# State updates of the linear attention as two half-tile products over four chunks

## The reference

```python
def gla_chunked(q, k, v, g, s0):          # per chunk of 16 tokens
    b = jnp.cumsum(g, axis=2)
    q_dec, k_inv = q * jnp.exp(b), k * jnp.exp(-b)
    k_end = k * jnp.exp(b_last - b)
    a = jnp.where(causal, jnp.einsum('bnihk,bnjhk->bnhij', q_dec, k_inv), 0.0)
    o_intra = jnp.einsum('bnhij,bnjhv->bnihv', a, v)
    def step(s, xs):
        o = jnp.einsum('bihk,bhkv->bihv', qd, s)
        s = s * dec[..., None] + jnp.einsum('bjhk,bjhv->bhkv', ke, vv)
        return s, o
    ...
```

## Time and profile before

| | us |
|---|---|
| median of 3 runs | 3917.28 (3915.54 to 3919.32) |
| profiled execution, device time | 3916.27 |
| its span in the profile | 3914.5 |
| TensorE busy in it | 3387.8 (87%) |
| VectorE busy | 2694.3 (69%) |
| ScalarE busy | 2125.3 (54%) |
| GpSimd busy | 572.5 (15%) |

### The profile page before, as it was taken

The page is one execution under the profiler, slowest core; times in us unless marked ns, Lnnn a source line. Parts: engine busy times, 40 slices in busy tenths (PEclk is TensorE's granted clock), DMA queues, the critical chain, the costliest instruction groups (busy, mean ns, idle before and its releaser), DMA issues. The chain is left out here.

```text
span 3914.5 us, 50754 instructions
## 1 busy us (share of the span) xinstructions
PE 3387.8 (87%) x17144; PEld 2769.9 (71%) x17144; DVE 2694.3 (69%) x3836; ACT 2125.3 (54%) x2780; POOL 572.5 (15%) x286
## 2 busy tenths in 40 slices
PE   8869999957978999948888987999997888879997
PEld 6757777746766777737777676888776777568875
DVE  3669999966668999976865656774565555555545
ACT  3539999943538999953444623332234445634433
POOL 0005333410004334420020300000000011300000
PEclk9879999978979999978989888999998989789998
DMA  3149999942048999953320032331331210022222
GB/s 111 49 152 396 419 418 410 407 180 94 12 164 356 419 416 416 412 200 117 104 70 2 1 108 100 117 117 65 113 105 50 58 61 1 3 80 96 93 84 81
DMA packets 148091, 651.33 MB, mean 166 GB/s; under 512 B 23478, under 2 KB 36968, under 8 KB 89448
## 3 DMA queue, kind: packets, MB, share of 16 engines
q1 hardware_dynamic: 137576, 631.59, 42.6%
q0 software_dynamic: 10080, 16.80, 1.1%
q10 hardware_dynamic: 288, 1.05, 0.1%
HBM read 645.01 MB, written 24.26 MB: 171 GB/s over the span
## 5 line engine op out<-in xcount | busy, mean ns | idle before, releaser
L1762 DVE TENSOR_TENSOR w_low<-w_raw,w_high 128x2048 fp32r<-128x2048 f32 x392 | 881.9, 2282 | 55.5 <-ACT w_high L1759 51.2
L1759 ACT CAST w_high<-w_raw 128x2048 fp32r<-128x2048 f32 x392 | 746.1, 1910 | 77.5 <-DMA w_raw<-in_moe_gate_dram 33.8
L2069 PE MATMUL banks<-w_high,x_split 128*128 128x512 f32 x1024 | 421.0, 411 | 46.6 <-DVE w_low L1762 39.1
L2069 PE MATMUL banks<-w_low,x_split 128*128 128x512 f32 x1024 | 407.8, 398 | 0.0
L529 PE MATMUL banks<-w_high,x_high 128*128 128x512 f32 (+2 forms) x808 | 309.6, 383 | 57.4 <-DVE w_low L435 31.5
L399 ACT CAST w_high<-w_raw 128x512 fp32r<-128x512 f32 (+2 forms) x200 | 117.8, 589 | 427.1 <-PE banks L529 421.2
L3376 PE MATMUL banks<-x_high,w_high 128*128 128x512 f32 (+1 forms) x1056 | 320.9, 358 | 21.2 <-DVE w_low L3414 21.2
L3376 PE MATMUL banks<-x_high,w_low 128*128 128x512 f32 (+1 forms) x1056 | 324.0, 361 | 0.0
L3376 PE MATMUL banks<-x_low,w_high 128*128 128x512 f32 (+1 forms) x1056 | 320.1, 357 | 0.0
L529 PE MATMUL banks<-w_high,x_low 128*128 128x512 f32 (+2 forms) x808 | 300.3, 372 | 0.0
L529 PE MATMUL banks<-w_low,x_high 128*128 128x512 f32 (+2 forms) x808 | 300.3, 372 | 0.0
(11 more groups left out here) (410 smaller groups left out, 7241.4 us busy)
## 6 DMA issues: line engine op xcount, KB each, us to landing
w_raw<-in_moe_gate_dram SPq DMA_DIRECT2D x132, 1024.0 KB, 10.5
w_raw<-in_moe_up_dram SPq DMA_DIRECT2D x132, 1024.0 KB, 10.2
w_raw<-in_moe_down_dram SPq DMA_DIRECT2D x132, 1024.0 KB, 10.9
w_raw<-in_ffn_w_up_dram SPq DMA_DIRECT2D x44, 1024.0 KB, 4.9
w_raw<-in_ffn_w_down_dram SPq DMA_DIRECT2D x88, 256.0 KB, 2.7
modulation<-in_w_adaT_dram SPq DMA_DIRECT2D x42, 512.0 KB, 4.2
hiddenT<-in_w_adaT_dram SPq DMA_DIRECT2D x28, 512.0 KB, 3.7
w_raw<-in_w_cols_dram SPq DMA_DIRECT2D x48, 256.0 KB, 2.9
```

What stands on the lines that cost most here:

```text
L1759: act.copy(ex["WS"][0][:, v % HIGH, :], ex["WR"][:, v % RAW, :]).then_inc(ex["high"], 1)
L1762: dve.tensor_tensor(ex["WS"][1][:, v % LOW, :], ex["WR"][:, v % RAW, :], ex["WS"][0][:, v % HIGH, :].bitcast(F32), ALU.subtract).then_inc( ...
L2069: ins_ = pe.matmul(GU[b][m], stationary(b, kk), WS[w][:, s, k * BANK:(k + 1) * BANK], start=(kk == 0 and w == 0), stop=(kk == KD - 1 and w ...
```

## The change

The widened values have four chunks in place of eight: the new table `half_chunk` marks, on each partition, the chunk's number within its half of the tile (chunks 0 to 3 on partitions 0 to 63, and 4 to 7 as 0 to 3 on 64 to 127). An update is now two matmuls: partitions 0 to 63 into one bank, 64 to 127 into the next, each with 256 moving columns. Only the second one signals `updates`. Further:

- `UB(n)` is a pair of half-filled banks of 0 to 3, so `BR` is 2; `VX` has 6 buffers of half the size.
- VectorE evacuates direction 0 of n % 3 != 2, that is two halves of three n; ScalarE four.
- VectorE widens only n = 0, ahead of the loop; GpSimd all others, and its three `block_q` come behind all widenings.
- `place` copies from two banks, with four chunks of each.

```diff
+    parts["half_chunk"] = (np.arange(P)[:, None] // CHUNK % 4 == np.arange(4)[None, :]) * 1.0
-        VR, BR, SR = 3, 4, 4
+        VR, BR, SR, NC4 = 6, 2, 4, P // CHUNK // 2
-            VX = spare[:, 0:VR * NC8 * GLA_DV].rearrange("p (r c v) -> p r c v", r=VR, v=GLA_DV)
+            VX = spare[:, 0:VR * NC4 * GLA_DV].rearrange("p (r c v) -> p r c v", r=VR, v=GLA_DV)
-            UB = lambda n: self.ps[0:2 * GLA_DK, n % BR, :]
+            UB = lambda n: self.ps[0:2 * GLA_DK, n % BR * 2:n % BR * 2 + 2, 0:NC4 * GLA_DV]
-            by_dve = lambda n, d: d == 0 and n % 3 == 0
+            by_dve = lambda n, d: d == 0 and n % 3 != 2
-            from_pool = lambda n: n % 3 != 2
+            from_pool = lambda n: n > 0
-                eng.tensor_tensor(VX[:, n % VR], V(n // HG, n % HG).unsqueeze(1).broadcast_to([P, NC8, GLA_DV]),
-                                  self.const("chunk").unsqueeze(2).broadcast_to([P, NC8, GLA_DV]),
+                eng.tensor_tensor(VX[:, n % VR], V(n // HG, n % HG).unsqueeze(1).broadcast_to([P, NC4, GLA_DV]),
+                                  self.const("half_chunk").unsqueeze(2).broadcast_to([P, NC4, GLA_DV]),
-                return copy(dst, UB(n)[d * GLA_DK:(d + 1) * GLA_DK].rearrange("p (c v) -> p v c", v=GLA_DV))
+                return copy(dst.rearrange("p v (b c) -> p v b c", b=2),
+                            UB(n)[d * GLA_DK:(d + 1) * GLA_DK].rearrange("p b (c v) -> p v b c", v=GLA_DV))
-                        if t % 2 == 1:
-                            pool.wait_ge(expanded[0], expands((t + 1) * HG - 2))
-                            block_q(pool.tensor_copy, 0, t // 2).then_inc(blocked, 1)
-                            pool.wait_ge(blocked, t // 2 + 1)
+                    pool.wait_ge(expanded[0], expands(N - 1))
+                    for hh in range(HG):
+                        block_q(pool.tensor_copy, 0, hh).then_inc(blocked, 1)
+                        pool.wait_ge(blocked, hh + 1)
-                        pe.matmul(UB(n), KE[:, n // HG, grp * HG + n % HG].rearrange("p d k -> p (d k)"),
-                                  VX[:, n % VR].rearrange("p c v -> p (c v)"), start=True, stop=True).then_inc(updates, 1)
+                        for b in range(2):
+                            half = slice(b * P // 2, (b + 1) * P // 2)
+                            ins_ = pe.matmul(UB(n)[:, b], KE[half, n // HG, grp * HG + n % HG].rearrange("p d k -> p (d k)"),
+                                             VX[half, n % VR].rearrange("p c v -> p (c v)"), start=True, stop=True)
+                        ins_.then_inc(updates, 1)
-                    expand(dve, 2)
+                    expand(dve, 0)
-                            if n + 3 < N:
-                                expand(dve, n + 3)
```

## The result

| | before | after |
|---|---|---|
| median, us | 3917.57 (3909.57 to 3919.32, 6 runs) | 3891.32 (3888.75 to 3898.29, 6 runs) |
| profiled execution, us | 3916.27 | 3897.15 |
| its span, us | 3914.5 | 3895.3 |

The ratio is 0.9941, with an interval of 0.9929 to 0.9952.

The account below looks back on a forecast made before the run. TensorE was taken to set the pace of the four stages, ScalarE 0.2 us behind. Stage gains of 17.0 us, less 0.9 and 1.2, left 14.9: 3916.3 - 14.9 = 3901.4 us, range 3897 to 3915.

Parts of the forecast that it names:

- The four more constants' columns cost nothing that a row could show.: Constants table: its four added columns were taken to have no visible cost.
- Halves side by side, 0.43 us.: State update on TensorE: two 64-row products overlap, taking 0.43 us at 2.4 GHz instead of 0.86 in a row.
- Rival 3: Half overlap: the second half waits for the first's second pass, 0.64 us a pair; 3909.5 us, chance 0.08.
- The circle: Warm tile: slowest dependency loop, update, scores, three masks, next evacuation on VectorE, next update; 3.04 us instead of 3.38.
- ScalarE's circle: Warm tile: the loop through ScalarE's four evacuations, 2.54 us, below the loop through VectorE.
- Widenings and q copies hidden.: GpSimd: three half widenings of 0.52 us a tile, and q copies of 1.0 to 1.5 us each, delay nothing.
- The evacuations from two banks: Copies out of the paired banks: no change taken, 0.62 and 0.67 us, though 0.1 more each was not excluded.
- The first tile: Cold start of each stage at half clock: loop of 3.66 us, update 5 starting 6.47 us after the stage's start.
- the second stage has some 0.45 less to give: Second stage of each layer: 1.4 us less at half clock, so 0.45 us less gain each, 0.9 in all.
- All of it should reach the end.: Behind the stages: the whole 14.9 us gain arrives at the kernel's end, since nothing late waits there.
- Rival 2: TensorE's clock stays at 1.2 GHz: no stage gain, and products behind start at half rate; 3927 us, chance 0.08.
- Rival 1: The update's halves run one after the other: warm loop 3.47 us, total 3915 to 3918, no difference; chance 0.14.

Follow-up runs that it names:

- pad4: The kernel before with the four half_chunk columns added to its constants table and nothing that uses them; 3901.49 us, ratio 0.9970.
- samewidth: The whole change, but half_chunk takes the place and width of the unused table chunk, so no tile moves; 3910.66 us, ratio 0.9980 to before.
- masks21: The changed kernel with VectorE's order as two masks, the next tile's first evacuation, then the third mask; 3887.53 us, ratio 0.9923 to before.
- acts5: The changed kernel with the moved evacuation given back, so ScalarE does five and VectorE one; 3899.35 us, ratio 0.9974 to before.
- after_again: The changed kernel run once more, unaltered, on the same chip as the other runs; 3894.74 us, ratio 0.9947 to before.

## Why the prediction was wrong, step by step

*"The four more constants' columns cost nothing that a row could show."* This step failed, and it is the miss. They cost nothing where they are read, but move each tile behind them, and 17.7 of the 26 us come from there (pad4). The forecast thought of reading four more columns, and not of a longer table that moves the tiles behind it. With this term taken out, the rest was too high: 8.6 us (samewidth) where 14.9 were forecast. The two misses pull against each other: 17.7 us of gain are missing and 6.3 are too many, so the total is nearer than its parts, by luck.

*Halves side by side, 0.43 us.* Right. From the start of the third update to the scores it takes 2147.33 - 2146.75 = 0.58 us, and 0.43 + 0.09 + 0.05 were summed. Rival 3's 0.64 for a pair would give 0.78: the second half doesn't wait for the first half's second pass.

*The circle.* Right, 3.10 for 3.04: VectorE's order last, with no idle time behind the masks. masks21 and acts5 move it by what the terms say. ScalarE's circle, next in line, was summed too low: 2.54 for the 2.77 of masks21, with no wait in it. The wake of TensorE was 0.08 for 0.05.

*Widenings and q copies hidden.* Right, though a half widening takes 0.61 us on GpSimd where half of 1.04 was taken; the copies take 0.86 each and end 4.5 us ahead of the scans. The evacuations from two banks are unchanged, 0.62 and 0.69.

*The first tile, and "the second stage has some 0.45 less to give".* Wrong in size. In the first stage, where the clock rises as assumed, the first mask follows its scores 1.26 us later (2140.53 to 2141.79) where 0.95 was taken, and the stage comes out at 21.79 for 21.59. In the second stages it was assumed that the clock rises as far into them as before. In after it rises 8.8 us into the second stage of layer 0 and 9.0 into that of layer 1, where the earlier trace rows had 5.4 in the former:

```profile
2199.60:2208.00 8.40, 7.68 (x42) 3.63 (x45) 4.46 (x9) 5.04 (x8) 6.15 (x11) 0.50 0.01 2
2208.50:2221.70 13.20, 10.06 (x99) 4.69 (x96) 10.17 (x23) 10.29 (x18) 6.08 (x9) 1.00 0.00 1
2222.10:2225.10 3.00, 2.92 (x14) 2.96 (x15) 3.00 (x2) 2.95 (x4) 0.00 (x0) 0.50 0.00 0
```

The stage starts at 2199.36. Over the runs of the changed stage its length goes with the rise: 20.7 us with a rise at 4.1 us, 21.2 at 6.5, 22.1 at 9.0, 22.3 at 10.5 (all layer 1). In the second stages 1.2 and 1.8 us are missing from the forecast, 3.0 of the 3.9 missing in all. Where the rise falls is not the change's doing alone: in pad4, whose stages are those of before, the first comes at 4.0 us and the stage is 24.16 us instead of 25.51.

*"All of it should reach the end."* Wrong. The third line above shows it: behind the second stage the clock falls again, for the 128-column products at L3127. In after_again and samewidth it does behind the first stage too, and then, of the 4.1 us that this stage is shorter, only 2.3 arrive at the start of the second (start to start 64.0 us against 66.27 before); in the profile of after, without that fall, 3.5 of 3.7 do (62.77). In acts5, with a fall, 1.5 of 2.9 arrive; in masks21, without one, 4.8 of 5.0. So 1.4 to 1.8 us are lost behind a first stage with a fall and 0.2 behind one without. Before has one fall, behind its fourth stage; samewidth has three, two more. Its stages are 12.1 us shorter and 8.6 arrive: the difference is 3.5. That is near two falls, but it rests on one profile of each kernel, and which stages have a fall changes between runs of one kernel. In the profile of after the count doesn't come out: it has one fall as before has, and 4.3 us are missing. Of these 1.9 are missing behind the fourth stage, where from its start to the end kernels with the stage of before take anything from 544.8 to 548.5 us. So that a gain is lost behind the stages is shown, and its size by falls only behind the first. Rival 2 had named this cost, but as all or nothing.

*Rival 1* was priced at no difference, 3915 to 3918. Both kernels that bring it about take 3971 to 3974. It had left out that 64 rows at a time don't get the full clock: rivals 1 and 2 are one.

## What to carry to other kernels

A kernel that waits for large weights from DRAM can depend on where its ring starts: try a multiple of 256 bytes, and when a change makes a tile longer, list which tiles move before comparing times. Split a change's gain with a kernel that has only its side effect, here unused columns, before crediting the change. Where two half products run side by side, the gain is what the next circle leaves (here VectorE's masks ahead of an evacuation), and a ring cut from four to two brings that circle in.

## What the runs showed of the hardware

- 1 MB loads into a ring at a multiple of 256 bytes land in 9.7 to 10.5 us (median by weight tensor) where the same at 224 past it take 10.2 to 10.9; in two stages bound by such loads that is 12 to 18 us of 3917. A start at 64 or 128 past it gives only 3.8 and 5.3.
- Two products in rows 0 to 63 and 64 to 127, into two banks, start together: four records within 0.3 us, 0.43 us for the pair at 2.4 GHz. The Trainium skill, "TensorE: Matmul & The Clock Gate", "The mechanism", keeps starts and ends of products in program order. Nothing here speaks against it for whole products; but the passes of an fp32 product don't keep the next strip waiting. Two passes of one half would start 0.213 us apart, and all four of a pair start within 0.27, so the second half's first one starts ahead of the first half's second one.
- TensorE busy without a gap on 64 of its rows stayed at 1.2 GHz for 33.5 us; with both halves at once and waits in between it had 2.4 (busy 10.06 us of the 13.20 above).
